# Feed-forward layers of a fused decoder trunk: narrow and wide products alternate instead of rows of two

## The reference

```python
def conv_ffn(h, w_up, conv_w, conv_b, w_down):
    u = jnp.einsum('bsd,df->bsf', h, w_up)          # 2048 -> 2 * 5632
    ...                                             # causal depthwise conv of width 3 on u
    val, gate = jnp.split(y, 2, axis=-1)
    return jnp.einsum('bsf,fd->bsd', jax.nn.silu(gate) * val, w_down)   # 5632 -> 2048

def reference(x, ...):
    for l in range(DEPTH):
        h = rms_norm(x, mix_norm[l])
        x = x + (parallel_mixer(h, ...) if l % 2 == 0 else pool_mixer(h, ...))
        h = rms_norm(x, ffn_norm[l])
        x = x + conv_ffn(h, w_up[l], conv_w[l], conv_b[l], w_down[l])
    return rms_norm(x, final_norm)
```

## Time and profile before

| | us |
|---|---|
| median of 3 runs | 1969.96 |
| lowest and highest | 1969.05, 1971.29 |
| the profiled execution's own time | 1971.31 |
| its span, first to last instruction | 1969.2 |
| TensorE busy | 1946.8 |
| TensorE weight loads busy | 1695.7 |
| VectorE busy | 1390.2 |
| ScalarE busy | 1110.4 |

### The profile page before, as it was taken

How to read it: one execution, slowest core, us unless ns; L and a number is a source line. 1 busy time by engine, 2 the same in 40 slices (tenths; PEclk the granted TensorE clock), 3 DMA queues, 4 the chain that set the end, 5 groups by cost and what they waited for, 6 DMA issues and landing times.

```text
span 1969.2 us, 31335 instructions
## 1 busy us (share of the span) xinstructions
PE 1946.8 (99%) x11094; PEld 1695.7 (86%) x11094; DVE 1390.2 (71%) x2149; ACT 1110.4 (56%) x1844; POOL 48.2 (2%) x53
## 2 busy tenths in 40 slices
PE   8999999999999999999999999999999999999998
PEld 8888888888888888888888887888888888888887
DVE  6667776767777777777655555877777777755555
ACT  6555545556656656656555546666566566645554
POOL 0002240000000000000000000000000000000000
PEclk9999999999999999999999998999999999999999
DMA  9654545555555555555565553555555555545653
GB/s 321 193 171 159 183 161 163 190 192 189 185 185 190 192 192 187 184 185 186 175 214 187 183 186 114 186 190 192 192 187 184 185 190 192 192 166 185 207 191 107
DMA packets 205202, 364.91 MB, mean 185 GB/s; under 512 B 6563, under 2 KB 49100, under 8 KB 205132
## 3 DMA queue, kind: packets, MB, share of 16 engines
q1 hardware_dynamic: 203388, 362.34, 55.2%
q10 hardware_dynamic: 1744, 1.63, 0.3%
HBM read 361.83 MB, written 2.11 MB: 185 GB/s over the span
## 4 chain that ended last, share of the span: by engine, by line
PE 96%; DVE 2%; ACT 1%; DMA 0%; SPq 0%; issue 0%; DVEq 0%
PE ps L386 53%; PE ps L389 26%; PE ps L444 7%; PE ps L448 3%; PE ps L478 2%; PE ps L481 2%; PE ps L480 2%; DVE lo L1092 1%; DMA raw<-in_w_in 0%; ACT hi L737 0%; PE ps L462 0%; PE ps L465 0%; PE ps L464 0%; PE ps L585 0%; PE ps L571 0%
## 5 line engine op out<-in xcount | busy, mean ns | idle before, releaser
L1092 DVE TENSOR_TENSOR lo<-raw,hi 128x512 fp32r<-128x512 f32 x1360 | 926.2, 697 | 522.3 <-ACT hi L737 517.7
L737 ACT ACTIVATE hi<-raw 128x512 fp32r<-128x512 f32 x1352 | 842.9, 630 | 800.9 <-PE ps L389 666.3
L386 PE MATMUL ps<-h,hi 128*128 128x512 f32 x2816 | 887.0, 396 | 4.8 <-DVE x L1399 3.3
L389 PEld LDWEIGHTS ps<-h,lo 128*128 128x128 f32 x2816 | 530.1, 188 | 125.5
L389 PE MATMUL ps<-h,lo 128*128 128x256 f32 x2816 | 554.1, 278 | 0.0
L386 PE MATMUL ps<-act,hi 128*128 128x512 f32 x1392 | 437.2, 395 | 0.0
L386 PEld LDWEIGHTS ps<-h,hi 128*128 128x128 f32 x2816 | 429.8, 189 | 5.8 <-DVE x L1399 3.5
L389 PEld LDWEIGHTS ps<-act,lo 128*128 128x128 f32 x1392 | 261.5, 188 | 61.8
L389 PE MATMUL ps<-act,lo 128*128 128x256 f32 x1392 | 273.4, 278 | 0.0
L386 PEld LDWEIGHTS ps<-act,hi 128*128 128x128 f32 x1392 | 211.9, 189 | 0.0
L444 PE MATMUL ps<-h,hi 128*128 128x512 f32 x576 | 183.5, 400 | 0.9 <-DVE lo L1092 0.9
(11 more groups left out here) (175 smaller groups left out, 1108.5 us busy)
## 6 DMA issues: line engine op xcount, KB each, us to landing
raw<-in_w_up SPq DMA_DIRECT2D x176, 1024.0 KB, 5.0
raw<-in_w_down SPq DMA_DIRECT2D x88, 1024.0 KB, 5.1
raw<-in_w_in SPq DMA_DIRECT2D x54, 1024.0 KB, 5.1
raw<-in_w_out SPq DMA_DIRECT2D x16, 1024.0 KB, 5.0
raw<-in_pool_w SPq DMA_DIRECT2D x4, 1024.0 KB, 5.3
raw<-in_w_in SPq DMA_DIRECT2D x8, 256.0 KB, 5.8
x<-in_xT SPq DMA_DIRECT2D x8, 128.0 KB, 4.8
x<-in_xT SPq DMA_DIRECT2D x2, 512.0 KB, 8.5
```

The source lines that it names most:

```text
L386: pe.matmul(ps[:, bank + m, :], hi[:, kt, m * P:(m + 1) * P], mv, start=first and kt == 0, stop=False, skip_group_check=True)
L389: mm = pe.matmul(ps[:, bank + m, S:2 * S], lo[:, kt, m * P:(m + 1) * P], mv[:, 0:S], start=False, stop=last and kt == KT - 1, skip_group_c ...
L737: a_.activation(hi[:, kt, :], raw[:, slot, kt, :], ACT.Copy).then_inc(hi_done, 1)
L1092: ve.tensor_tensor(lo[:, kt, :], raw[:, slot, kt, :], hi[:, kt, :].bitcast(F32), ALU.subtract).then_inc(lo_done, 1)
```

## The change

The up- and down-projections of both layers call a new helper, `swapped_unit`, in place of `wide_unit`. In it the two products of a column tile stand together: narrow m=0, wide m=0, narrow m=1, wide m=1 and so on. In the first k-tile of a column group it is wide, narrow for each m. The `w_used` count sits on the k-tile's last matmul as before, which is now a wide one except in a group's first k-tile. `last_unit` alternates in the same way in all four k-tiles, and its `tail_mm` count moves to the wide product of the last k-tile. The last narrow products no longer carry `stop`. The output projection of the attention keeps `wide_unit`, and the other helpers are as they were.

```diff
+            def swapped_unit(n, base, bank, first, moving, ready=None):
+
+                for kt in range(KT):
+                    pe.wait_ge(lo_done, base + KT * n + kt + 1)
+                    if ready is not None:
+                        ready(kt)
+                    mv = moving(kt)
+                    clears = first and kt == 0
+
+                    def wide(m):
+                        return pe.matmul(ps[:, bank + m, :], hi[:, kt, m * P:(m + 1) * P], mv, start=clears, stop=False,
+                                         skip_group_check=True)
+
+                    def narrow(m):
+                        return pe.matmul(ps[:, bank + m, S:2 * S], lo[:, kt, m * P:(m + 1) * P], mv[:, 0:S],
+                                         start=False, stop=False, skip_group_check=True)
+                    for m in range(4):
+                        if clears:
+                            wide(m)
+                            mm = narrow(m)
+                        else:
+                            narrow(m)
+                            mm = wide(m)
+                    mm.then_inc(w_used, 1)
+
             def last_unit(n, bank):
...
                 pe.wait_ge(lo_done, KT * n + 1)
-                for row in (0, 2):
-                    for m in (row, row + 1):
-                        wide(0, m)
-                    for m in (row, row + 1):
-                        narrow(0, m, False)
+                for m in range(4):
+                    narrow(0, m)
+                    wide(0, m)
                 pe.wait_ge(lo_done, KT * (n + 1))
                 for m in range(4):
-                    wide(1, m)
-                    wide(2, m)
-                    narrow(1, m, False)
-                    narrow(2, m, False)
-                    wide(3, m)
-                    narrow(3, m, True).then_inc(tail_mm, 1)
+                    for kt in range(1, KT):
+                        narrow(kt, m)
+                        mm = wide(kt, m)
+                    mm.then_inc(tail_mm, 1)
...
-                            wide_unit(U_UP[l] + 4 * gt + j, i * (8 * KT), wide_bank(G), j == 0, j == UP_UNITS - 1,
-                                      lambda kt: h[:, KT * j + kt, :], split if first and gt == 0 else None)
+                            swapped_unit(U_UP[l] + 4 * gt + j, i * (8 * KT), wide_bank(G), j == 0,
+                                         lambda kt: h[:, KT * j + kt, :], split if first and gt == 0 else None)
...
-                        wide_unit(U_DN[l] + DN_UNITS * half + j, i * (2 * DN_UNITS * KT), wide_bank(G), j == 0,
-                                  j == DN_UNITS - 1, lambda kt: act[:, KT * j + kt, :])
+                        swapped_unit(U_DN[l] + DN_UNITS * half + j, i * (2 * DN_UNITS * KT), wide_bank(G), j == 0,
+                                     lambda kt: act[:, KT * j + kt, :])
```

More of the change, by code:

```diff
@@ L393, in last_unit @@
             def last_unit(n, bank):
                 def wide(kt, m):
[L396 to L401, removed]
@@ L403, in last_unit, with narrow @@
-                pe.wait_ge(lo_done, KT * n + 1)
-                for row in (0, 2):
-                    for m in (row, row + 1):
-                        wide(0, m)
-                    for m in (row, row + 1):
-                        narrow(0, m, False)
+                    return pe.matmul(ps[:, bank + m, :], hi[:, kt, m * P:(m + 1) * P], act[:, KT * (DN_UNITS - 1) + kt, :],
+                                     start=False, stop=False, skip_group_check=True)
+                def narrow(kt, m):
+                    pe.matmul(ps[:, bank + m, S:2 * S], lo[:, kt, m * P:(m + 1) * P],
+                              act[:, KT * (DN_UNITS - 1) + kt, 0:S], start=False, stop=False, skip_group_check=True)
```

## The result

| | before | changed |
|---|---|---|
| median, us | 1970.14 (4 runs) | 1984.59 (4 runs) |
| lowest and highest, us | 1969.05, 1971.29 | 1981.73, 1985.44 |
| ratio, 95% interval | | 1.0073, 1.006 to 1.0085 |
| span of the profiled execution, us | 1969.2 | 1983.3 |

What follows compares the result with a forecast made beforehand. TensorE's matmul start-to-start distance was taken to bound the kernel. Alternation at 350.2 against 348.3 ns over 4224 pairs gave +8 us, all else nothing: 1978 us against the 1969.96 us median, range 1961 to 1986 us.

Steps and rivals of the forecast that it cites:

- What bounds the kernel: TensorE, busy 99% of the span and almost never waiting; 4224 feed-forward pairs at 348.3 ns, 4.2 us per nanosecond.
- What the order costs (the main term): Alternation in the feed-forward k-tiles and last unit takes 350.2 instead of 348.3 ns per pair, +8 us.
- the round trip is what costs the 3.3 ns: Each change from wide to narrow and back costs 3.3 ns, so an alternating pair takes 350.0 ns, +7 us.
- the mixture in the old last unit: Old last unit's wide wide narrow narrow wide narrow averaged 350.6 ns per pair; alternation no worse would mean +9.5 us.
- The bounds: Limits for an alternating pair: 346.7 ns below (7 us saved) and 352.5 ns above (+18 us).
- uniform sum: Settled wide-only step of 226.7 ns plus narrow-only step of 120.0 ns, 346.7 ns per pair if type changes are free.
- upper bound: Four purely alternating pairs at the tile ends of the old last unit, mean 352.5 ns, +18 us.
- rival 1: Alternation settles at 346.7 ns per pair in every feed-forward k-tile, -7 us, 1963 us; chance 0.28 including cheaper.
- Rival 3: Alternation costs what its own four pairs in the old last unit show, 352.5 ns, +18 us, 1988 us; chance 0.18 including dearer.
- Rival 2: Order makes no difference: 348.3 ns per pair stays, about 1970 us; chance 0.22 together with the change not taking effect.
- Release of the buffers, dropped flags, last unit: ScalarE gets `hi` some 8 ns later, covered, cost 0; flags cost nothing; closing chain under 0.1 us.
- What would show it: Down-projection's 688 pairs take 240.9 us, steps about 118 and 232 ns; feed-forward idle about 5 us; attention part unchanged.

Runs made afterwards that it cites:

- rows of four: Changed kernel with each feed-forward k-tile as four wide, then four narrow products: 1978.25 us median, ratio 1.0043.
- strict kernels: Changed kernel with the wide product first in every feed-forward k-tile, or the narrow first in every one: medians 1963.90 and 1964.21 us.
- turning k-tile: Strictly alternating narrow-first kernel with one k-tile of layer 1's up-projection as wide narrow narrow wide narrow wide narrow wide: 1962.57 us median, ratio 0.9971.
- rows of two: Order of the kernel before the change, two wide then two narrow products in a set: 1970.14 us median, 348.3 ns per pair in the down-projection.

## Why the prediction was right, and where it was not

**What bounds the kernel**: right. TensorE stayed without waits, one nanosecond per pair was worth 4.2 us, and the whole effect is 3.4 ns per pair (14.4 us / 4224).

**What the order costs (the main term)**: the sign was right and the size was short, +8 us against +14.4. The step that failed is the choice of one rate: the term of 1.9 ns per pair measured 3.4 ns, and as a mean of two rates. I took 350.2 ns, between "the round trip is what costs the 3.3 ns" and the mixture in the old last unit. The first reading is refuted by the rows of four, which have fewer round trips and cost 350.5 ns. The second averaged over something that isn't an average: with hindsight 350 ns is about halfway between the two rates that alternation has, 346.7 and 353.3 ns. So the sign, and a time inside the stated range, were in part luck: the true number hung on the share of the slow rhythm, which no row of before could give, (351.7 - 346.7) / 6.6 or about three quarters. That share hung on the place in the cycle at which a group of 64 pairs ends. The strict kernels, with the same alternation and no break, had medians of 1964 us and could not be told from the kernel before.

**The bounds**: both were nearly met as such. The uniform sum, 346.7 ns, is exactly the fast rhythm; the upper bound of 352.5 ns, from four pairs, lies just under the slow rhythm's 353.3 ns. The fault was to treat them as bounds of one unknown value instead of as two states.

**Rivals**: rival 1 (alternation settles at the uniform sum) is true wherever the engine is in the fast rhythm, and for the whole kernel once the turning k-tile is in; its 1963 us is what that version measures. Rival 3 (the dear pairs taken at their word, 1988 us) is what the changed kernel comes near: 1984.6 us is closer to it than to the forecast's 1978 us. Rival 2 falls: the same columns in the same number, with the same weight loads, go by at 346.7, 348.3, 350.5 or 353.3 ns per pair. The Trainium skill's formula by which the distance depends on the columns alone (TensorE: Matmul & The Clock Gate, section "Back-to-back issue gap") does not give these: it makes 325 ns of each. The Trainium skill calls it, in that section, the gap of an isolated matmul, and says that in a stream of weight loads and matmuls both set the spacing.

**Release of the buffers, dropped flags, last unit**: right, all at nothing. ScalarE's wait stayed in the hundreds of microseconds, and the last unit's 16 pairs run at the fast rate but for one wait on `lo` and the few pairs behind it.

**What would show it**: the changed rhythm showed in the timeline as announced, but as 233, 241 and 236 ns behind a wide product instead of one value. The feed-forward part of layer 0 began at 441.6 us, against 441.8 us before, so nothing ahead of it had changed. The forecast's own range, 1974 to 1983 us, was missed; the wide one, up to 1986 us, held.

## What to carry to other kernels

Where TensorE runs without waits, compare the start-to-start steps over a full period of the order, in several places, before settling on a mean: one instruction order can have more than one steady rate, and a mean of two rates predicts neither. If the times of a kernel fall into two clusters, look for the place behind which the traces part, here the last wait of a layer, and put the experiment there; a single k-tile was worth 0.65%. And an order that needs an exception (here the first k-tile) should be tried without it, since the exception itself can be what costs: here 13 of 20 executions without it came out 5 to 9 us below the kernel before, though the other seven came out 5 to 8 us above it.

## What the runs showed of the hardware

- Alternating a 512-column and a 256-column matmul, each with its own weight load, has a fast rhythm at 346.7 ns per pair and a slow one at 353.3 ns, which repeats every three pairs with 20 ns lost per cycle. Neither ended without a disturbance of the order or a wait, over as many as 2000 pairs. Which rhythm a disturbance leads to depends on its pattern, on the rhythm ahead of it and on the place in that rhythm's cycle. One pattern was met 28 times and another 42 times out of the slow rhythm in one trace each, and at the same place it never ended differently.
- The period of three fits neither the four column tiles, nor the k-tile, nor the four banks, nor a semaphore count (once per four pairs), and operands are the same in both rhythms. That points to TensorE's own handling of the loads and streams, by exclusion only; which part of the engine holds that state is not shown by any record here and stays open. In all alternating kernels the two products of a pair go into one bank, one behind the other. The fast rhythm shows that this costs nothing by itself, but no run alternates between banks, so whether the slow rhythm needs it is not shown.
- At granted clock 0.50 (1216 to 1220 us of the kernel before) the next start comes 427 ns behind a wide product and 213 ns behind a narrow one, 1.28 us for a set of two and two. At clock 1.00 the uniform streams take 226.7 and 120.0 ns, 13 ns more than half of these. At clock 1.00 rows of four cost more (350.5 ns) than rows of two (348.3 ns), which cost more than alternation in the fast rhythm (346.7 ns).
